# The first projection in two halves of its channels, ordered around the four modulation weights

## The reference

```
for i in range(2):
    sh, sc, gt = split(silu(c) @ w_mod[i] + b_mod[i], 3)        # and sh_c, sc_c, gt_c from c_ctx
    h_lat = x * (1 + sc) + sh
    h_ctx = ctx * (1 + sc_c) + sh_c
    mixer(h_lat, h_ctx)            # block 0: attention with latent q and kv; block 1: state space (S5)
```

## Time and profile before

| what | value |
|---|---|
| median of 3 runs | 1725.0 us (1724.32 to 1728.8) |
| the profiled execution | 1723.97 us, its span 1722.2 us |
| mean granted TensorE clock | 0.974 of full |
| PE busy | 1592.3 us, 92% of the span |
| DVE busy | 729.9 us, 42% |
| ACT busy | 365.0 us, 21% |

### The profile page before, as it was taken

The page is one execution under the profiler, slowest core; times in us unless marked ns, Lnnn a source line. Parts: engine busy times, 40 slices in busy tenths (PEclk is TensorE's granted clock), DMA queues, the critical chain, the costliest instruction groups (busy, mean ns, idle before and its releaser), DMA issues.

```text
span 1722.2 us, 23309 instructions
## 1 busy us (share of the span) xinstructions
PE 1592.3 (92%) x9548; PEld 1044.9 (61%) x9548; DVE 729.9 (42%) x1543; ACT 365.0 (21%) x850; POOL 99.9 (6%) x176
## 2 busy tenths in 40 slices
PE   3999989999998959989988999998899989899999
PEld 2555556666554555566677888863445554588853
DVE  4799745555689863672770101103101212133310
ACT  0222233332211231123221000000214431221100
POOL 1022210000022220000110000000000000000000
PEclk8999999999998979999999999999999999899999
DMA  9755760500885654375762444454343122355431
GB/s 308 188 172 188 240 222 1 144 16 1 278 249 158 211 205 146 123 258 200 280 238 105 147 147 157 160 186 156 130 139 107 49 98 98 103 161 160 162 135 61
DMA packets 200331, 270.75 MB, mean 157 GB/s; under 512 B 51263, under 2 KB 118305, under 8 KB 198945
## 3 DMA queue, kind: packets, MB, share of 16 engines
q1 hardware_dynamic: 145840, 201.08, 34.9%
q10 hardware_dynamic: 43249, 42.80, 7.5%
q0 software_dynamic: 11136, 25.37, 4.4%
HBM read 226.16 MB, written 42.99 MB: 156 GB/s over the span
## 4 chain that ended last, share of the span: by engine, by line
PE 65%; issue 15%; DVE 11%; DMA 5%; ACT 2%; POOL 1%; ACTq 1%; POOLq 0%; DVEq 0%
PE bank L431 62%; PE bank L434 3%; DMA mc_scratch<-memory 3%; DMA memory<-in_b_mod 1%; DMA memory<-mc_scratch 1%; DVE memory L1823 1%; DVE memory L1834 1%; DVE memory L1826 1%; DVE memory L1827 1%; DVE memory L1830 1%; DVE memory L1832 1%; POOL memory L2310 1%; DVE memory L1850 1%; DVE memory L1843 1%; DVE memory L1846 1%
## 5 line engine op out<-in xcount | busy, mean ns | idle before, releaser
L431 PE MATMUL bank<-memory 128*32 128x128 f32 (+8 forms) x8784 | 1499.8, 367 | 58.0 <-issue 16.3
L431 PEld LDWEIGHTS bank<-memory 128*128 128x128 f32 (+3 forms) x8784 | 949.5, 161 | 565.3 <-issue 454.6
L434 PE MATMUL bank<-memory 128*128 128x128 f32 (+1 forms) x764 | 112.5, 295 | 67.9 <-DVE memory L2183 16.9
L434 PEld LDWEIGHTS bank<-memory 128*128 128x128 f32 (+1 forms) x764 | 97.1, 152 | 107.2 <-issue 57.1
L2303 POOL DMA_DIRECT2D k_scratch<-memory x128 | 76.0, 602 | 536.9 <-ACT memory L1219 535.4
L2266 DVE SCALAR_TENSOR_TENSOR memory<-bank,memory 128x255 f32<-128x255 f32 x44 | 21.0, 478 | 113.7 <-ACT memory L1577 113.7
L2110 DVE TENSOR_TENSOR memory<-memory 128x256 f32<-128x256 f32 x56 | 23.2, 415 | 99.6 <-ACT memory L1399 99.6
L1209 ACT ACTIVATE memory<-bank 128x512 f32<-128x512 f32 x64 | 34.9, 596 | 121.5 <-PE bank L434 114.7
L2159 DVE TENSOR_SCALAR memory<-bank,memory 128x256 f32<-128x256 f32 x16 | 6.6, 477 | 120.5 <-PE bank L431 120.5
L1949 DVE TENSOR_REDUCE memory<-bank 128x1 f32<-128x512 f32 (+1 forms) x48 | 30.2, 684 | 61.9 <-PE bank L431 61.9
L1302 ACT ACTIVATE memory<-bank,memory 128x512 f32<-128x512 f32 (+1 forms) x64 | 36.3, 580 | 85.5 <-DVE memory L1952 85.5
(11 more groups left out here) (240 smaller groups left out, 915.3 us busy)
## 6 DMA issues: line engine op xcount, KB each, us to landing
memory<-in_s_w_glu SPq DMA_DIRECT2D x16, 2048.0 KB, 9.1
memory<-in_w_mod SPq DMA_DIRECT2D x12, 2048.0 KB, 13.5
memory<-in_w_ffn_up SPq DMA_DIRECT2D x22, 1024.0 KB, 7.7
memory<-in_w_in SPq DMA_DIRECT2D x10, 2048.0 KB, 7.9
mb_scratch<-memory ACTq DMA_DIRECT2D x32, 512.0 KB, 3.2
mc_scratch<-memory ACTq DMA_DIRECT2D x32, 512.0 KB, 5.0
memory<-mb_scratch SPq DMA_DIRECT2D x32, 512.0 KB, 4.6
memory<-mc_scratch POOLq DMA_DIRECT2D x32, 512.0 KB, 6.3
```

The lines of the kernel that those rows point to most:

```text
L431: return nc.tensor.matmul(o, l, r, start=start, stop=stop, skip_group_check=free)
L434: return nc.tensor.transpose(o, i, ident[0:n, 0:n])
```

## The change

The order of the modulation tiles becomes 0, 2, then 1, 3. With tiles 0 and 2 the shift and scale of channels 0 to 511 are known. Half of the transposes (k2 = 0, 1), half of the modulation and half of each token tile's accumulation (`head_part(t, 0)`, 4 of 8 channel tiles) are done from them. Between those, tiles 1 and 3 are multiplied and turned; then the second half follows, `head_part(t, 4)`. The transposes of `lamT`, the small row and `c_in` stay behind t = 0 and t = 2, now of the second pass. The `poles()` steps on DVE are dealt out differently: 6, 6, 26, 12, and what remains after the second half's modulation; before they were 12, 18, 22, 8 and the remainder.

The load list changes as well. Before: mod 0, 1, 2, 3, head, gate 0, 1, 2, mod 4, gate 3, mod 5. After: mod 0, 2, head, mod 1, 3, gate 1, 0, 2, mod 4, gate 3, mod 5. SP issues them in that order, but gate 0 ahead of gate 1. Each waits for the load three places ahead of it in the list.

```
-        for ct in range(4):
-            mod_load(0, ct)
+        mod_load(0, 0)
+        mod_load(0, 2)
         load("head_in", ...)
-        for ct in range(4):
+        mod_load(0, 1)
+        mod_load(0, 3)
+        for ct in (1, 0, 2, 3):
             load(("gate", ct), ..., ("gate_mm", 4 * ct + 3))
             if ct >= 2:
                 mod_load(0, 2 + ct)
...
+            mod_product(0, 0, 1)
+            mod_product(0, 2, 2)
+            mod_turned(0, 0, 3)
             for c in range(2):
-                x_transposes(0, c)
-            w = weights(pe, "head_in", (KD, HEAD_IN))
+                x_transposes(0, c, 0, 4 + 2 * c)
+            mod_turned(0, 2, 0)
+
+            def head_part(t, k0):
+                w = weights(pe, "head_in", (KD, HEAD_IN))
+                if k0 == 0:
+                    bank(pe, ("head", t), [("ckv", t), ("qn", t), ("kr", t)], 4 + t)
+                for k in range(k0, k0 + 4):
+                    last = mm(banks[4 + t][:, 0:HEAD_IN], hT[:, k, t * P:(t + 1) * P], w[:, k, :], k == 0, k == KD - 1)
+                if k0:
+                    last.then_inc(*S.up("head_mm", t))
+
             for c in range(2):
-                modulated_ready(0, c)
+                modulated_ready(0, c, 0, 2)
+            for t in range(2):
+                head_part(t, 0)
+            mod_product(0, 1, 0)
+            for t in range(2, 4):
+                head_part(t, 0)
+            mod_turned(0, 1, 1)
+            mod_product(0, 3, 2)
+            x_transposes(0, 0, 2, 0)
+            mod_turned(0, 3, 3)
+            x_transposes(0, 1, 2, 2)
+            for c in range(2):
+                modulated_ready(0, c, 2, 4)
             for t in range(NTT):
-                b = bank(pe, ("head", t), [("ckv", t), ("qn", t), ("kr", t)], 4 + t)
-                for k in range(KD):
-                    last = mm(b[:, 0:HEAD_IN], hT[:, k, t * P:(t + 1) * P], w[:, k, :], k == 0, k == KD - 1)
-                last.then_inc(*S.up("head_mm", t))
+                head_part(t, 4)
                 if t == 0:
                     pe.wait_ge(*S.at("lam_ready"))
...
             dve.wait_ge(*S.at("lam_in"))
-            advance(12)
-            mod_row(0, 0)
-            advance(18)
-            mod_row(0, 1)
-            mod_columns(0, 0)
-            advance(22)
-            mod_row(0, 2)
-            mod_columns(0, 1)
-            advance(8)
-            mod_row(0, 3)
-            mod_columns(0, 2)
-            mod_columns(0, 3)
-            for c in range(2):
-                modulated(0, c)
+            advance(6)
+            mod_row(0, 0)
+            advance(6)
+            mod_row(0, 2)
+            mod_columns(0, 0)
+            mod_columns(0, 2)
+            for c in range(2):
+                modulated(0, c, (0,))
+            advance(26)
+            mod_row(0, 1)
+            mod_columns(0, 1)
+            advance(12)
+            mod_row(0, 3)
+            mod_columns(0, 3)
+            for c in range(2):
+                modulated(0, c, (2,))
             advance(100)
             dve.wait_ge(*S.at("lamT_mm"))
```

More of the change, by code:

```diff
@@ L416, in at_bank, with row_, row_user @@
             return banks[places.get(key, 0)]
+        def row_(l, ct):
+            return (0, 0, 1, 1, 0, 1)[ct] if l == 0 else ct % 2
+        def row_user(l, ct):
+            if l == 0:
+                return {0: None, 2: None, 1: (0, 0), 3: (0, 2), 4: (0, 1), 5: (0, 3)}[ct]
+            return (l, ct - 2) if ct >= 2 else (l - 1, ct + 4)
         def modulate_views(l, k, c):
@@ L452, in mod_turned @@
                 pe.wait_ge(*S.at("mod_row", (l, ct)))
-                tr(b[:, 0:P], modrow[:, ct % 2, :]).then_inc(*S.up("modT_mm", (l, ct)))
+                tr(b[:, 0:P], modrow[:, row_(l, ct), :]).then_inc(*S.up("modT_mm", (l, ct)))
             def gate_rows(l):
@@ L463, in gate_rows, with x_transposes @@
                         last.then_inc(*S.up("gtb_mm", (l, n, c)))
-            def x_transposes(l, c):
-                for k2 in range(KD // 2):
-                    b = bank(pe, ("xT", l, c, k2), [("hT_v" if k2 % 2 == 0 else "hT_a", (l, c, k2))], 4 + k2 if l else None)
+            def x_transposes(l, c, k0=0, i0=4):
+                for k2 in range(k0, k0 + 2) if l == 0 else range(KD // 2):
+                    b = bank(pe, ("xT", l, c, k2), [("hT_v" if k2 % 2 == 0 else "hT_a", (l, c, k2))], i0 + k2 - k0)
                     for i in range(2):
@@ L473, in x_transposes, with modulated_ready @@
                     last.then_inc(*S.up("xT_mm", (l, c, k2)))
-            def modulated_ready(l, c):
-                for k2 in range(KD // 2):
+            def modulated_ready(l, c, k0=0, k1=KD // 2):
+                for k2 in range(k0, k1):
                     pe.wait_ge(*S.at("hT_v" if k2 % 2 == 0 else "hT_a", (l, c, k2)))
@@ L1159, in gate_rows, with modulated @@
                         A(gtb[:, c, n * 512:(n + 1) * 512], at_bank("gtb", l, n, c), ACT.Copy).then_inc(*S.up("gtb", (l, n, c)))
-            def modulated(l, c):
-                act.wait_ge(*S.at(*(("folded",) if l else ("shsc", (l, 3)))))
-                for k2 in range(1, KD // 2, 2):
+            def modulated(l, c, k2s=(1, 3)):
+                for k2 in k2s:
+                    act.wait_ge(*S.at(*(("folded",) if l else ("shsc", (l, 2 + k2 // 2)))))
                     act.wait_ge(*S.at("xT_mm", (l, c, k2)))
@@ L1169, in modulated @@
                     ins.then_inc(*S.up("hT_a", (l, c, k2)))
+            for c in range(2):
+                modulated(0, c, (1,))
             act.wait_ge(*S.at("theta"))
@@ L1175, in _ @@
             for c in range(2):
-                modulated(0, c)
+                modulated(0, c, (3,))
             def c_conjugated(q, ql):
@@ L1610, in mod_row @@
                 dve.wait_ge(*S.at("bmod"))
-                if ct >= 2 or l:
-                    dve.wait_ge(*S.at("modT_mm", (l, ct - 2) if ct >= 2 else (l - 1, ct + 4)))
-                tt(modrow[:, ct % 2, :], at_bank("mod", l, ct)[:, 0:P], bmod[:, 6 * l + ct, :], ALU.add).then_inc(*S.up("mod_row", (l, ct)))
+                if row_user(l, ct):
+                    dve.wait_ge(*S.at("modT_mm", row_user(l, ct)))
+                tt(modrow[:, row_(l, ct), :], at_bank("mod", l, ct)[:, 0:P], bmod[:, 6 * l + ct, :], ALU.add).then_inc(*S.up("mod_row", (l, ct)))
             def mod_columns(l, ct):
@@ L1618, in mod_columns, with modulated @@
                 ts(shsc[:, l, 4 * ct:4 * ct + 4, :], i, 1.0 if 2 <= ct < 4 else 0.0, None, ALU.add).then_inc(*S.up("shsc", (l, ct)))
-            def modulated(l, c):
-                dve.wait_ge(*S.at(*(("folded",) if l else ("shsc", (l, 3)))))
-                for k2 in range(0, KD // 2, 2):
+            def modulated(l, c, k2s=(0, 2)):
+                for k2 in k2s:
+                    dve.wait_ge(*S.at(*(("folded",) if l else ("shsc", (l, 2 + k2 // 2)))))
                     dve.wait_ge(*S.at("xT_mm", (l, c, k2)))
@@ L2368, in ring @@
                 ring_load(load_no[key])
-            for ct in range(4):
-                ring(("mod", 0, ct))
+            ring(("mod", 0, 0))
+            ring(("mod", 0, 2))
             ring("head_in")
+            ring(("mod", 0, 1))
+            ring(("mod", 0, 3))
             b_load(0)
             c_load(0)
-            for ct in range(4):
+            for ct in (0, 1, 2, 3):
                 ring(("gate", ct))
```

## The result

The change made the kernel slower: 1733.29 us median of 9 runs (1730.27 to 1738.06) against 1725.0 us of before in the same measurement, ratio 1.0045 with a 95% interval of 1.003 to 1.0059. A second measurement on another occasion gave 1734.17 against 1726.75, 1.0042 (1.0027 to 1.0057). That is 7.4 to 8.3 us where 4.3 were forecast. The profiled execution has a span of 1732.7 us.

What follows compares the result with a forecast made beforehand. PE is busy most of the span, but DVE's chain meets it at banks 4 and 5 with 0.3 us slack. Bank lateness 2.7 plus clock 1.6 gave 4.3 us on 1725.0, so 1729.3 us, range 1724 to 1733.

Steps and rivals of the forecast that it cites:

- the transposes of the first half: On PE ahead of the head: 16 token transposes and tile 2's row, 17 at 0.12 us each, ending at 28.9.
- the steps of the poles ahead of tile 3's row: On DVE before the second half: taken as done by then, with 0.3 us for tile 3's row beside 8 transposes.
- the chain's lateness: DVE's chain from the turned poles' copy to the banks: 3.0 us late, bounds 1.1 to 5.5.
- First half: From the bias's landing at 26.19, transposes at full clock and modulation; PE begins the head at 31.3.
- Up to the second half: First-half head tiles with 1.9 us lost to clock, then products of tiles 1 and 3; second half begins at 53.1.
- The poles: 14 steps left behind the second half's modulation, 5.1 us; PE waits some 2 us, poles' copy at 58.8 against 55.77.
- PE's gain and its loss at the banks: Gates start 6.0 us early at about 68.8; PE waits for bank 5 until 98.6, 2.7 us late against 95.88.
- Clock: Behind PE's idle time of about 7 us, half clock on the gate matmuls costs 1.6 us, bounds 0.5 and 2.6.
- What follows: After the banks: DVE's 3.3 us wait at unit 4 goes; the last store wait moves with PE and keeps its length.
- The store behind 4 MB: Rival at unit 8: unit 5's store takes 17 to 19 us; free up to 19.5, at 22 total 1733; chance 0.11.
- PE setting the end: Rival: DVE's delay is swallowed and the whole 6.0 us gained, 1719.0; chance of faster 0.07.

Runs made afterwards that it cites:

- Late_norm_first: Kernel before with 14 extra small DVE copies behind the poles' copy and the latents' normalization moved ahead of units 0 and 1; 1727.67 us against 1727.59.
- pe_filled: Changed kernel with gate block 2 computed a second time, result unused, to keep PE busy in its wait; 1735.15 us against 1727.8 for the kernel before.
- after: The changed kernel itself, first measurement, against the kernel before; 1733.29 us against 1725.0, ratio 1.0045.
- after_again: The changed kernel measured once more on another occasion, against the kernel before; 1734.17 us against 1726.75, ratio 1.0042.
- poles_early: Changed kernel with the poles' steps dealt out 6, 6, 38, 14, none left over; 1730.02 us against 1727.8 for the kernel before.
- loads_apart: Changed kernel with the load of gate 3 issued ahead of that of modulation tile 4; 1733.54 us against 1727.8 for the kernel before.
- dve_late: Kernel before with only 14 small copies added on DVE right behind the copy of the turned poles; 1731.2 us against 1727.8, ratio 1.0026.
- both: Changed kernel with the changes of lamt_early and norm_first together; 1718.59 us against 1726.75 for the kernel before, ratio 0.9951.
- lamt_early: poles_early with the poles also turned and copied ahead of the product of tile 3; 1724.65 us against 1726.75 for the kernel before.
- norm_first: Changed kernel with the latents' normalization moved ahead of units 0 and 1 on DVE, poles still late; 1728.47 us against 1726.75 before.

## Why the prediction was right, and what of it was off

The direction, the place and the links from DVE's late chain to the banks and the clock were right. The size was too small: 1733.29 us lies 0.3 above the upper bound of 1733, and 4.0 above the value of 1729.3. The outcome, slower by more than 0.3%, had been given 0.36, and within 0.3% 0.57. The terms that were too small are the transposes of the first half, the steps of the poles ahead of tile 3's row, and with them the chain's lateness.

- *First half.* The head's start was forecast for 31.3 and came at 30.82, and its 96 instructions took 16.04 us, 2.0 over what 32 at 0.375 and the product in 2.0 take at full clock; 1.9 was the term for it. The term that failed is the one in front, "17 at 0.12 us each at full clock". It holds for the first trace (18 in 2.18 us). In the eight others they took 1.4 us more or longer, and the head began at 32.1 to 33.2. The chain has this delay in full.
- *Up to the second half.* Forecast 53.1, measured 54.11 and 56.48. A small term was missing: 12 steps of the poles stood in front of `mod_row(0, 3)` and ended only at 50.9, so the row of tile 3 came 2 us after its product, and PE waited 1.5 us for it (the idle time before the group at 51.39). I had counted these steps as done in earlier gaps; DVE's order puts them behind `mod_columns(0, 1)`, for which it waits until 47.0.
- *The poles.* 14 steps, 5.1 us, a wait of PE ahead of the transposes: as forecast. Chain 3.0 us late, within 1.1 to 5.5: measured 3.85, and 5.6 on the mean of the other four traces with this order of the poles, just past that bound. Here is most of the 3 to 4 us by which the sum is short.
- *PE's gain and its loss at the banks.* Gates early by 6.0 us forecast; the row at 66.66 holds 8 instructions of the head, 3.0 us, so they began at 69.7, 5.2 us early. Waited away in full. Bank 5 was forecast for 98.6, measured 99.57. Late_norm_first shows the mechanism by taking it away.
- *Clock.* 1.6 us forecast; the gate block took 1.7 us more and the four transposes ahead of it 0.4, and pe_filled gets these back at that place. How much reaches the end isn't resolved. In four traces with half clock behind the wait (after, after_again, poles_early, loads_apart) the mark is 1.2 to 1.9 us later, against before, than bank 5 is; in dve_late, at full clock, it is 0.5 less; but in pe_filled, also at full clock, it is 1.4 more. The forecast had the clock at 1.00 during the idle time, as in the earlier trace rows; it was 0.50 in its last 4 us.
- *What follows.* The store behind PE's gate block 11 moved with PE (15.34 us at 182.23, against the earlier trace rows); DVE waited for it 4.85 us, 7.80 before. DVE's wait at unit 4 vanished.
- *The rivals.* The store behind 4 MB took 17.0 us, as estimated, and by the traces cost nothing. Unit 8 began at 161.96, within the forecast for the store's landing. The DMA engines take turns between the queues packet by packet, as the Trainium skill (DMA: Bandwidth & Descriptors, section Queues, rings and completion order) states it. The trace agrees: 453 packets against 455 from 155 to 158 us. My reading of that rule was wrong: I made equal shares of bytes of it, twice the 5.0 us of the earlier trace rows, about 10. Turns by packet are not equal shares when one queue's packets are four times as large, and so 12.0, 15.7 and 17.0 us say nothing against the rule. PE setting the end was wrong for this kernel, and right for `both`, which takes away what stood against it.

How far each of the later clock stretches adds to single executions (10.5 us between the two spans, 5.6 to 8.8 at 250 us) stays open. They differ from run to run within one kernel.

## What to carry to other kernels

Before an engine is made to arrive earlier, look for the place where it next meets another engine, and measure the slack there: here it was 0.3 us at two PSUM banks, 45 us behind the change. A chain on the other engine that fills the old gaps has to be dealt out again, the critical steps first, and what is not yet needed (here two units of work) belongs behind the reads that free a bank. With both done, 7 to 8 us slower became 7 to 8 us faster. And where two queues share the DMA engines, a transfer in small packets gets few of the bytes, here a fifth.

## What the runs showed of the hardware

TensorE's level behind an idle time was not the same each time: behind 2.27 and 0.93 us (dve_late) a gate block took 7.03 us, behind 3.22 and 0.50 (lamt_early) 7.54, behind 3.90 (norm_first) 8.76, behind 7.6 (after, after_again) 8.68 and 8.39. Which of the two levels a short burst of work early in the kernel gets differs between executions of the same kernel: the same 18 transposes of the changed kernel took 2.18 and 3.85 us. A change that puts such a burst on the critical path takes on that spread.

Two DMA queues with work took turns by packet: 453 packets of ACT's store against 455 of SP's loads in 3 us, which is 0.23 MB against 0.93. A 512 KB store in packets of 0.5 KB took 4.2 us alone and 17.0 behind 4 MB of loads.
